# A hybrid RG-LRU and mLSTM step: the next x projection ahead of the gates, and a setup whose loads don't wait

## The chip, the core and the metric

One core of a Trainium2 chip runs the whole step as one program. The metric is the device time of that program in microseconds; smaller is better.

## What is computed

Two layers on 128 context and 1024 latent tokens of 1024 channels, in float32. The change touches the first layer's start and its recurrence only:

```python
def rms_norm(x, g):
    return x * lax.rsqrt(jnp.mean(x * x, axis=-1, keepdims=True) + EPS) * g
def ada_mod(cond, w, b):                       # w: (1024, 3072)
    return jnp.split(jax.nn.silu(cond) @ w + b, 3)      # shift, scale, gate
h = rms_norm(x, g_pre) * (1 + scale) + shift   # cond: c for latents, c_ctx for context
xa, za, xb, zb = jnp.split(h @ w_in, 4)        # 1024 columns each
xa = centred_dwconv(xa, conv_w, conv_b)        # 4 taps along the tokens
for d in range(2):                             # forward, backward
    r = sigmoid(block_diag(xa, w_r[d]) + b_r[d]); i = sigmoid(block_diag(xa, w_i[d]) + b_i[d])
    log_a = -8 * r * softplus(-lam[d]); a = exp(log_a)
    u = sqrt(-expm1(2 * log_a)) * (i * xa)     # + a * h0 at the first latent token
    h_t = a_t * h_{t-1} + u_t; ya += h
y = concat(ya * silu(za), fourier(xb) * silu(zb)) @ w_out
```

The Fourier mixer (a two-dimensional DFT of xb in groups of 128 channels, and a small product), the output projection and the second layer (mLSTM) follow.

## The kernel before

Everything lies with channels on the 128 partitions and the 1152 tokens along the free dimension. Each engine has its own instruction list; they meet at semaphores that are waited for by constants worked out.

**Projections.** A float32 product is made of three: weights and activations are split into a high and a low part, and `project` (lines 114 to 127) issues 72 matmuls (8 slices of 128 channels, 3 combinations, 3 groups of 384 tokens) into one of two groups of three PSUM banks. A weight tile of 1024x128 goes through two slots: SP loads it (`w_load`, line 94) once the tile before in that slot is split, ScalarE makes the high part (`w_split_hi`, line 100), VectorE the low part (`w_split_lo`, line 107). The tiles have one fixed order, in pairs.

**Setup** (`setup`, lines 218 to 395). SP loads x in nine tiles of 128 tokens through four slots, then w_mod in eight slices of 128 rows by 2048 columns through four slots, so it waits for the use of a slot (lines 247 and 257); then two weight tiles, the store of the transposed x to DRAM, and 13 vectors with one element per partition. ScalarE issues nine more such loads (lines 316 to 322) before its first operation. TensorE transposes x tile by tile, ScalarE and VectorE copy it to `xT`. ScalarE squares `xT` by channel slices (line 184), TensorE adds the squares up over the channels into three strips of 32 PSUM rows (line 194), root and reciprocal follow, and line 201 spreads the result over the partitions. The modulation (silu(c) and silu(c_ctx) times w_mod) is made in two ways: six slices by VectorE, which multiplies a slice by a column of the condition and adds it to a sum (line 367), two by TensorE with w_mod as the stationary operand and two moving columns (line 301); 32 + 32 one-column products add VectorE's sums over the partitions (line 307). VectorE multiplies x by the inverse deviation (line 374), adds bias and gains to the modulation (lines 377 to 381); ScalarE and VectorE then modulate x and split it (lines 216, 343, 390, 393), and the first projection follows slice by slice. A barrier of all engines ends the setup.

**Recurrence** (`lru`, lines 430 to 655): eight blocks of 128 channels. In block i TensorE projects x into group 0 and z into group 1, waits for the convolution and makes the gates, r then i for each direction (lines 507 to 524); a gate is three matmuls of 385 columns, in float32, which the profile counts as six instructions. ScalarE copies x out of PSUM (lines 545 to 547), makes the high part of a weight, takes z out by a tanh and a half (lines 552, 553) once GpSimd has finished the block before, evacuates the gates (557, 560), makes the decay (566), the tanh (570) and a square (573), splits a weight and takes two roots (584). VectorE makes the product of z (626), per direction two products (630, 632), then per direction a product and two scans (637, 640), and at the end convolves the next block's x in four operations (613, 615). GpSimd waits for the scans, adds the two directions and multiplies by z (463, 468), stores the result, and before that loads the next gate weights.

**Hand-over.** The Fourier stage (`fourier`, lines 658 to 927) has the same engines go on. TensorE projects xb of its group 0, turns it to tokens, projects zb, projects xb of group 1 and makes the token transform of group 0 (line 751), for which it waits for VectorE's eight-point butterflies. VectorE makes these after a first share of the remaining modulation (`add_modulation`, line 868), whose w_mod rows SP loads once GpSimd has finished the last block of the recurrence (line 693).

## Time and profile before

| | us |
|---|---|
| median of 3 runs | 2283.5 (2279.87 to 2286.92) |
| profiled execution, whole | 2284.8 |
| its span | 2283.2 |
| TensorE busy | 2115.9 (93%) |
| setup, to the barrier | about 104 |
| recurrence, to the last gate | 104 to 404 |

Busy times are shares of the span, and a busy TensorE is not one at its full clock: the granted clock of a stretch is given as a share of 2.4 GHz. A row of the timeline is a run of like instructions; what stands in brackets behind it is how long its engine had been idle and which instruction ended that. PE is TensorE, PEld its weight loads, DVE VectorE, ACT ScalarE, POOL GpSimd, SP the engine that issues most loads; a q behind a name stands for the engine's queue of issued work.

### The profile page before, as it was taken

The numbers are of one execution on the slowest core, as the hardware profiler recorded it, in microseconds if no ns is written. First come the engines' busy times: TensorE is split into PE (matmuls) and PEld (weight loads), VectorE is DVE, ScalarE is ACT, GpSimd is POOL, SyncE is SP. The second block draws the span as 40 slices with busy tenths as digits, with TensorE's granted clock in tenths as the row PEclk, the third lists the DMA queues.
The fourth block names the chain that finished last, engine by engine and source line by source line (L and its number), as shares of the span: only waits on it lengthen the run. The fifth ranks groups of instructions, "written<-read, shape, count | busy, mean of one in ns | idle before, by whom it ended". The sixth has DMA issues, their size and how long they took to land. (4 is left out here: it accounts for less than half of the span.)

```text
span 2283.2 us, 29516 instructions
## 1 busy us (share of the span) xinstructions
PE 2115.9 (93%) x12271; PEld 2020.3 (88%) x12271; DVE 1138.0 (50%) x1627; ACT 631.4 (28%) x710; POOL 147.0 (6%) x128
## 2 busy tenths in 40 slices
PE   5799898999999998858999999999999999989997
PEld 3778787899989998858999999999999999879997
DVE  4756666566866125666343433434343434553144
ACT  2356564421223224422121211112121211113242
POOL 0021313100000001200000000000000000000001
PEclk8699999999997999979999999999999999999998
DMA  7611111234254135312222031212222031342155
GB/s 215 163 47 47 53 47 53 66 127 133 67 169 165 41 101 164 129 46 80 70 75 63 19 110 37 90 49 83 63 75 63 26 106 33 79 175 77 56 153 179
DMA packets 235554, 205.09 MB, mean 90 GB/s; under 512 B 37306, under 2 KB 217018, under 8 KB 233266
## 3 DMA queue, kind: packets, MB, share of 16 engines
q1 hardware_dynamic: 219202, 191.07, 27.1%
q0 software_dynamic: 3680, 12.29, 1.5%
q10 hardware_dynamic: 12560, 0.12, 0.3%
q8 instruction: 85, 1.39, 0.3%
q14 instruction: 27, 0.22, 0.0%
HBM read 168.01 MB, written 35.29 MB: 89 GB/s over the span
## 5 line engine op out<-in xcount | busy, mean ns | idle before, releaser
L124 PE MATMUL psum_groups<-h_hi,w_hi 128*128 128x384 f32 x2280 | 530.9, 346 | 53.9 <-ACT q_t L1828 23.2
L124 PE MATMUL psum_groups<-h_lo,w_hi 128*128 128x384 f32 x2280 | 512.1, 337 | 0.0
L124 PE MATMUL psum_groups<-h_hi,w_lo 128*128 128x384 f32 x2088 | 480.3, 338 | 0.0
L124 PEld LDWEIGHTS psum_groups<-h_hi,w_hi 128*128 128x128 f32 x2280 | 410.9, 191 | 68.8 <-issue 37.3
L124 PEld LDWEIGHTS psum_groups<-h_lo,w_hi 128*128 128x128 f32 x2280 | 409.6, 190 | 0.0
L109 DVE TENSOR_TENSOR w_lo<-w_raw,w_hi 128x1024 fp32r<-128x1024 f32 x161 | 205.0, 1274 | 370.5 <-ACT w_hi L105 364.7
L124 PEld LDWEIGHTS psum_groups<-h_hi,w_lo 128*128 128x128 f32 x2088 | 377.3, 190 | 0.0
L105 ACT ACTIVATE w_hi<-w_raw 128x1024 fp32r<-128x1024 f32 x161 | 170.0, 1056 | 421.9 <-PE psum_groups L124 144.6
L1980 DVE SCALAR_TENSOR_TENSOR state<-state,head_decay,psum_extra 128x257 f32<-128x257 f32 x112 | 54.0, 482 | 289.4 <-PE psum_groups L1714 287.4
L1731 PE MATMUL psum_groups<-w_hi,h_hi 128*128 128x256 f32 x576 | 161.9, 281 | 2.8 <-ACT v_rows L1832 1.5
L1731 PE MATMUL psum_groups<-w_lo,h_hi 128*128 128x256 f32 x576 | 159.8, 277 | 0.0
L1731 PE MATMUL psum_groups<-w_hi,h_lo 128*128 128x256 f32 x576 | 159.8, 277 | 0.0
L145 PE MATMUL psum_groups<-h_lo,w_hi 128*128 128x384 f32 x432 | 119.0, 348 | 4.6 <-DVE w_lo L109 4.6
L145 PE MATMUL psum_groups<-h_hi,w_hi 128*128 128x384 f32 x432 | 117.1, 343 | 4.0 <-DVE h_lo L1374 2.1
L1731 PEld LDWEIGHTS psum_groups<-w_hi,h_hi 128*128 128x128 f32 x576 | 108.4, 188 | 4.8 <-ACT v_rows L1832 3.2
L1731 PEld LDWEIGHTS psum_groups<-w_hi,h_lo 128*128 128x128 f32 x576 | 108.4, 188 | 0.0
L1731 PEld LDWEIGHTS psum_groups<-w_lo,h_hi 128*128 128x128 f32 x576 | 108.2, 188 | 0.0
L522 PE MATMUL psum_groups<-xa_convolved,gate_weights 128*128 128x385 f32 x192 | 78.9, 574 | 27.3 <-DVE xa_convolved L615 23.9
L522 PEld LDWEIGHTS psum_groups<-xa_convolved,gate_weights 128*128 128x128 f32 x192 | 42.5, 226 | 61.2 <-DVE xa_convolved L615 26.1
L1083 POOL TENSOR_TENSOR square_sums<-square_sums,out_squares 128x1152 f32<-128x1152 f32 x6 | 16.0, 2674 | 1201.4 <-ACT out_squares L1238 1201.4
L1712 PE MATMUL psum_groups<-v_rows,decay_matrix 128*128 128x257 f32 x288 | 85.3, 382 | 3.5 <-DVE h_rows L1993 3.5
L1838 ACT ACTIVATE o_tanh<-psum_groups 128x1152 f32<-128x1152 f32 x16 | 18.1, 1131 | 252.3 <-PE psum_groups L124 252.3
(280 smaller groups left out, 2719.7 us busy)
## 6 DMA issues: line engine op xcount, KB each, us to landing
w_raw<-in_w_in_o SPq DMA_DIRECT2D x65, 512.0 KB, 4.4
w_raw<-in_w_in_e SPq DMA_DIRECT2D x32, 512.0 KB, 6.0
w_raw<-in_w_out_e SPq DMA_DIRECT2D x32, 512.0 KB, 3.9
w_raw<-in_w_out_o SPq DMA_DIRECT2D x32, 512.0 KB, 4.2
w_mod_rest<-in_w_mod SPq DMA_DIRECT2D x8, 1536.0 KB, 8.1
y_scratch<-mixed_y POOLq DMA_DIRECT2D x16, 576.0 KB, 5.9
h_hi<-y_scratch SPq DMA_DIRECT2D x8, 1152.0 KB, 8.8
h_lo<-y_scratch SPq DMA_DIRECT2D x8, 1152.0 KB, 15.5
```

Source lines behind the costliest of these rows:

```text
L105: act.activation(WHI[:, slot, :], WRAW[:, slot, :], ACT.Copy).then_inc(w_hi, 1)
L109: dve.tensor_tensor(WLO[:, slot, :], WRAW[:, slot, :], WHI[:, slot, :].bitcast(F32), ALU.subtract).then_inc(w_lo, 1)
L124: ins = pe.matmul(PS[:, group, j, 0:JW], w[:, slot, k * P:(k + 1) * P], h(k0 + k)[:, j * JW:(j + 1) * JW], start=start and k == 0 and m == ...
L145: ins = pe.matmul(bank, w[:, slot, k * P:(k + 1) * P], h(k0 + k)[:, g * JW:(g + 1) * JW], start=start and k == 0 and m == 0, stop=stop and ...
L522: ins = pe.matmul(PS[:, what, j, 0:JP], GW[:, 2 * what + d, :], XC[:, j * JP:(j + 1) * JP], start=True, stop=True)
L1083: pool.tensor_tensor(ACC[:], ACC[:], SQ[:].rearrange("p j n -> p (j n)"), ALU.add).then_inc(wide_added, 1)
L1712: ins = pe.matmul(NUM[d][:, 0:DV1], DM[q][:, d, cols], V[q][:, t, :], start=True, stop=s == 0)
L1731: ins = pe.matmul(dst, h[:, k, t * P:(t + 1) * P], w[:, slot, cols], start=k == 0 and m == 0 and n % 2 == 0, stop=k == KC - 1 and m == 2, ...
L1838: ins = act.activation(by_bank(TO[:]), group, ACT.Tanh, scale=0.5)
L1980: ins = dve.scalar_tensor_tensor(C[:, d, :], C[:, d, :], DC[:, d, tiles[d]:tiles[d] + 1], KV[d][:, 0:DV1], ALU.mult, ALU.add)
```

## The change

**Setup.** x gets nine slots (in the place of the later h_hi) and w_mod seven; SP issues all of x and seven slices without a wait, then the first weight tile, and the eighth slice after the first has been used. The vectors come as rows of 128 elements (five loads at the start for c, c_ctx, biases and gains; six in the middle of the squares for the recurrence), and TensorE turns each set in one transpose; SP issues none of them. ScalarE squares x by rows, with the sum over a row as a second result, right from the loaded tile; one root, one reciprocal, and nine products spread it. The modulation is TensorE's alone: for each slice four products with the two conditions (padded to 32 columns) as the stationary operand and 512 columns of w_mod as the moving one, each into its own strip of 32 PSUM rows; a copy by ScalarE and four transposes bring it to channels on partitions. VectorE's multiply-adds, the square sums on TensorE and the one-column products are gone.

**Recurrence.** TensorE projects z of block i, then x of block i + 1, then makes the gates of i, i before r in each direction. ScalarE takes out x of i + 1 at the start of block i, and z of i + 1 at its end, after the roots, into a new tile `z_tanh_a`; the tanh of the first direction waits for GpSimd's result of the block before. VectorE makes both i products, splits a weight, and puts the convolution of i + 1 between the two variances; its product of z now waits for GpSimd. Block 7 takes xb of the Fourier stage in the place of a next x, and the Fourier stage's first group projects zb ahead of the turn to tokens.

The core of the diff (most lines that go stand in the listing above and are left out here; semaphore names are changed elsewhere too):

```diff
+                src = a["x_prompt"][0] if t == 0 else a["x_sample"][0, (t - 1) * P:t * P, :]
+                sp.dma_start(XR[:, t, :], src).then_inc(x_in[t], 16)
             for n in range(KC):
                 if n >= WS:
...
+                    w_load(sp, 0, 0, in_tile(a["w_in_e"][0], 0))
+                    sp.wait_ge(wm_used, n - WS + 1)
                 sp.dma_start(WM[:, n % WS, :], wm_src[n][:, 0:2 * D]).then_inc(wm_in[n % WS], 16)
...
+            w_load(sp, 0, 1, in_tile(a["w_in_e"][0], D))
...
+            pe.wait_ge(x_rstd, 1)
+            pe.wait_ge(xT_act, 4)
+            for t in range(NT):
+                ins = pe.matmul(PS[:, 1, t // NJ, t % NJ * P:(t % NJ + 1) * P], STD[:, t:t + 1].to_broadcast([P, P]),
+                                IDENT[:], start=True, stop=True, skip_group_check=True)
+            ins.then_inc(x_spread, 1)
             pe.wait_ge(cond_ready, 1)
...
+            for k in range(KC):
                 pe.wait_ge(wm_in[k % WS], 16 * (k // WS + 1))
...
+                for j in range(4):
+                    ins = pe.matmul(PX[32 * j:32 * j + 32, 0, :], SCP[:, k, :], WM[:, k % WS, j * 512:(j + 1) * 512],
+                                    start=k == 0, stop=k == KC - 1)
                 ins.then_inc(wm_used, 1)
...
+            pe.wait_ge(mod_rows, 1)
...
+            for b in range(4):
+                ins = pe.transpose(PX[:, 1, b * P:(b + 1) * P], MR[:, b * P:(b + 1) * P], IDENT[:])
+            ins.then_inc(mod_turned, 1)
...
+                act.wait_ge(x_in[t], 16)
+                if t >= 2:
+                    act.wait_ge(x_summed, t - 1)
+                act.activation(SQ[:, t % 2, :], XR[:, t, :], ACT.Square, accum_out=SSQ[:, t:t + 1]).then_inc(x_summed, 1)
+                if t % 2 == 0 and t:
+                    x_copy(t - 1)
+            act.wait_ge(x_summed, NT)
+            act.wait_ge(zero_ready, 1)
+            act.activation(STD[:], SSQ[:], ACT.Sqrt, scale=1.0 / D, bias=EPSB[:]).then_inc(x_std, 1)
...
+            act.wait_ge(wm_used, KC)
+            act.activation(MR[:], PX[:, 0, :], ACT.Copy).then_inc(mod_rows, 1)
...
-            def block_of(i, first):
-                if not first:
-                    pe.wait_ge(r_out, i * 2)
-                    project(pe, i, 0, 0, hhi, hlo)
-                    pe.wait_ge(i_out, i * 2)
-                project(pe, i, 1, 1, hhi, hlo)
...
+            def gates(i):
                 pe.wait_ge(gw_in, i * 32 + 32)
                 pe.wait_ge(conv, i + 1)
                 for d in range(2):
...
+                    for what in (1, 0):
                         if what == 0:
...
+                            if d:
+                                pe.wait_ge(r_out, i * 2 + 1)
+                            elif isinstance(i, int) and i == KC - 1:
+                                pe.wait_ge(xb_out, 1)
+                            else:
+                                pe.wait_ge(x_out, i + 2)
                         else:
                             pe.wait_ge(*((i_out, i * 2 + 1) if d else (z_out, i + 1)))
                         for j in range(NJ):
...
                                             start=True, stop=True)
                         ins.then_inc(mm, 1)
...
+            def next_x(i):
+                project(pe, i, 0, 0, hhi, hlo)
+            project(pe, 0, 1, 1, hhi, hlo)
+            pe.wait_ge(x_out, 1)
+            next_x(1)
+            gates(0)
+            def block_of(i):
+                pe.wait_ge(i_out, i * 2)
+                project(pe, i, 1, 1, hhi, hlo)
+                pe.wait_ge(r_out, i * 2)
+                next_x(i + 1)
+                gates(i)
+            with pe.Fori(1, KC - 1) as i:
+                block_of(i)
+            block_of(KC - 1)
...
+            def z_evacuate(i, first=False):
                 projected(act, i, 1)
                 if not first:
...
+                    act.wait_ge(var1, i * 2)
+                act.activation(by_bank(ZT[:]), PS[:, 1, :, 0:JW], ACT.Tanh, scale=0.5)
                 act.activation(by_bank(ZH[:]), PS[:, 1, :, 0:JW], ACT.Copy, scale=0.5).then_inc(z_out, 1)
...
+                w_split_hi(act, i + 1, 1)
+            def block_of(i, first, last=False):
+                if last:
+                    projected(act, KC, 0)
+                    act.activation(by_bank(XB[:]), PS[:, 0, :, 0:JW], ACT.Copy).then_inc(xb_out, 1)
+                    w_split_hi(act, KC + 1, 0)
+                else:
+                    x_evacuate(i + 1)
+                if not first:
+                    act.wait_ge(scanned, i)
...
+                gate_i_out(0)
+                gate_r_out(0)
+                gate_i_out(1)
                 decay(0)
...
+                gate_r_out(1)
+                if not first:
+                    act.wait_ge(y_ready, i)
                 decay_squared(0)
                 decay(1)
                 decay_squared(1)
...
                 for d in range(2):
                     act.wait_ge(var1, i * 2 + 1 + d)
                     act.activation(T1[:, d, :], T1[:, d, :], ACT.Sqrt, scale=0.25).then_inc(root, 1)
...
+                if not last:
+                    z_evacuate(i + 1)
+            x_evacuate(0, True)
+            z_evacuate(0, True)
             block_of(0, True)
...
+            with act.Fori(1, KC - 1) as i:
                 block_of(i, False)
+            block_of(KC - 1, False, last=True)
...
+            w_split_lo(dve, 1, 0)
             convolve(0, first=True)
...
+            w_split_lo(dve, 1, 1)
+            before = ch.n
             def block_of(i, first, last=False):
...
                 dve.wait_ge(z_out, i + 1)
...
+                if not first:
+                    dve.wait_ge(y_ready, i)
+                ch.link(dve.scalar_tensor_tensor(GZ[:], ZT[:], 1.0, ZH[:], ALU.add, ALU.mult))
                 dve.wait_ge(conv, i + 1)
                 for d in range(2):
                     dve.wait_ge(i_out, i * 2 + 1 + d)
...
+                    ins = dve.scalar_tensor_tensor(T2[:, d, :], T2[:, d, :], 1.0, XC[:], ALU.add, ALU.mult)
+                ch.link(ins)
+                w_split_lo(dve, i + 2, 0)
+                for d in range(2):
                     dve.wait_ge(squared, i * 2 + 1 + d)
                     dve.scalar_tensor_tensor(T1[:, d, :], T1[:, d, :], 1.0, HT[:, d, :], ALU.add,
                                              ALU.mult).then_inc(var1, 1)
...
+                    if d == 0 and not last:
+                        convolve(i + 1)
...
             def group(i, m, slot, first):
                 channel_weights(m, slot)
+                if not first:
+                    pe.wait_ge(ua_out, i)
+                    project(pe, i + KC, 0, 0, hhi, hlo)
+                    token_transform(i - 1)
+                if first:
+                    pe.wait_ge(i_out, 2 * KC)
+                    project(pe, i + KC, 1, 1, hhi, hlo)
+                pe.wait_ge(xb_out, i + 1)
+                pe.wait_ge(cw_out, m * 2 + slot + 1)
                 if first:
                     pe.wait_ge(r_out, 2 * KC)
                 else:
...
                     pe.wait_ge(ub_out, i)
                 to_tokens(0, 6, lambda t: PS[:, 0, t // 2, t % 2 * 256:t % 2 * 256 + 256], ua_done)
                 to_tokens(6, 9, lambda t: PX[:, t // 2, t % 2 * 256:t % 2 * 256 + 256], ub_done)
...
+                if not first:
                     pe.wait_ge(y_ready, i)
...
+                    project(pe, i + KC, 1, 1, hhi, hlo)
```

## Rows read from the trace of the kernel before

**Rows 1.** The page, part 1: busy time and share of each engine.
```profile
PE 2115.9 (93%) x12271; PEld 2020.3 (88%) x12271; DVE 1138.0 (50%) x1627; ACT 631.4 (28%) x710; POOL 147.0 (6%) x128
```

**Rows 2.** Windows: busy us (instructions) per engine, granted clock, DMA share, GB/s.
```profile
27.00:34.00 7.00, 3.25 (x24) 2.57 (x24) 2.78 (x4) 2.24 (x3) 0.00 (x0) 1.00 0.92 327
...
34.00:44.00 10.00, 8.08 (x48) 1.50 (x48) 6.90 (x5) 9.40 (x9) 0.00 (x0) 0.83 0.98 407
...
48.00:60.00 12.00, 8.70 (x40) 7.54 (x37) 12.00 (x6) 0.00 (x0) 0.00 (x0) 0.50 0.42 143
...
88.00:104.00 16.00, 15.40 (x72) 14.97 (x72) 12.16 (x13) 11.80 (x12) 0.00 (x0) 0.82 0.00 1
...
129.50:156.00 26.50, 25.20 (x145) 24.88 (x144) 20.41 (x16) 13.97 (x14) 8.38 (x6) 1.00 0.10 30
```

**Rows 3.** Timeline of the setup: start, us, engine, line, operation, count, idle before.
```profile
47.57 18.09 DVE L367 SCALAR_TENSOR_TENSOR mod_sums<-w_mod_rows,cond_silu,mod_sums 128x2048 f32<-128x2048 f32 x8
...
69.04 13.79 PE L307 MATMUL psum_extra<-ones,mod_sums 128*128 128x1 f32 x64
...
83.59 1.62 ACT L216 ACTIVATE norm_tmp<-x_normed,mod_shift,mod_scale 128x128 f32<-128x128 f32 x2 [18.58 <-DVE mod_scale L381]
```

**Rows 4.** Timeline, ScalarE in the setup: a load's issue, a table load, a copy.
```profile
1.50 0.60 ACTq L317 DMA_DIRECT2D cond<-in_c_ctx  x1
...
17.51 1.28 ACT L324 ACT_TABLE_LOAD   x1 [17.51 <-issue]
...
24.39 1.02 ACT L327 ACTIVATE xT<-psum_groups 128x1024 f32<-128x1024 f32 x1 [4.46 <-PE psum_groups L288]
```

**Rows 5.** Groups by line, 0 to 560 us: busy us, mean ns, idle before.
```profile
L615 DVE SCALAR_TENSOR_TENSOR xa_convolved<-xa_padded,lru_params,xa_convolved 128x1155 f32<-128x1155 f32 x24 | 56.7, 2363 | 2.9 <-DVE xa_convolved L613 0.9 <-DVE xa_convolved L615 0.9
...
L640 DVE TENSOR_TENSOR_SCAN tanh_then_state<-decay,lru_params,gate_i 128x1024 f32<-128x1024 f32 x16 | 37.2, 2325 | 0.0
...
L109 DVE TENSOR_TENSOR w_lo<-w_raw,w_hi 128x1024 fp32r<-128x1024 f32 x26 | 33.4, 1284 | 30.1 <-ACT w_hi L105 30.1
...
L630 DVE SCALAR_TENSOR_TENSOR gate_i<-gate_i,xa_convolved 128x1155 f32<-128x1155 f32 x16 | 21.7, 1358 | 30.3 <-ACT gate_i L560 30.3
...
L374 DVE TENSOR_TENSOR x_normed<-xT,psum_groups 128x1152 f32<-128x1152 f32 x8 | 10.2, 1347 | 0.0
```

**Rows 6.** DMA issues, 0 to 130 us: count, KB each, median us to landing.
```profile
w_mod_rows<-in_w_mod SPq DMA_DIRECT2D x8, 1024.0 KB, 7.5
...
norm_gains<-in_g_post ACTq DMA_DIRECT2D x2, 4.0 KB, 4.0
```

**Rows 7.** Timeline of TensorE: squares' sums, gates after a project, gates after a wait.
```profile
39.86 0.85 PE L194 MATMUL psum_extra<-squares,ones 128*32 128x384 f32 x6 [0.21 <-ACT squares L184]
...
121.11 2.11 PE L522 MATMUL psum_groups<-xa_convolved,gate_weights 128*128 128x385 f32 x6
...
161.67 3.90 PE L522 MATMUL psum_groups<-xa_convolved,gate_weights 128*128 128x385 f32 x6 [3.17 <-ACT z_half L553]
```

**Rows 8.** Timeline of the recurrence: the convolution alone; GpSimd's sums and who waits.
```profile
113.78 4.34 DVE L615 SCALAR_TENSOR_TENSOR xa_convolved<-xa_padded,lru_params,xa_convolved 128x1155 f32<-128x1155 f32 x3
...
189.14 3.32 POOL L463 TENSOR_TENSOR tanh_then_state<-tanh_then_state 128x128 f32<-128x128 f32 x2 [17.52 <-DVE lru_final L642]
...
197.19 1.28 ACT L552 ACT_TABLE_LOAD   x1 [12.76 <-POOL mixed_y L468]
```

**Rows 9.** Timeline: the last block's gates and the hand-over to the Fourier stage.
```profile
393.95 9.73 PE L522 MATMUL psum_groups<-xa_convolved,gate_weights 128*128 128x385 f32 x24 [3.71 <-DVE xa_convolved L615]
...
423.14 3.72 POOL L463 TENSOR_TENSOR tanh_then_state<-tanh_then_state 128x128 f32<-128x128 f32 x2 [29.10 <-DVE lru_final L642]
...
429.39 25.33 SPq L686 DMA_DIRECT2D w_mod_rest<-in_w_mod  x4
...
438.09 2.35 DVE L868 TENSOR_SCALAR mod_by_partition<-w_mod_rest,cond_silu 128x4096 f32<-128x4096 f32 x1 [13.89 <-DMA w_mod_rest<-in_w_mod]
...
450.29 3.84 PE L751 MATMUL psum_groups<-token_dft,transformed 128*128 128x128 f32 x32 [2.87 <-DVE transformed L827]
```

More of the change, by code:

```diff
@@ L198, in spread_pe @@
-    def spread_pe(pe, n, group=0):
-        pe.wait_ge(rstd_ready, n + 1)
-        for j in range(NJ):
-            ins = pe.matmul(PS[:, group, j, 0:JW], ONES[32 * j:32 * j + 1, :], RSTD[32 * j:32 * j + 1, :],
-                            start=True, stop=True)
-        ins.then_inc(rstd_spread, 1)
-    def stats_dve(dve, n, used, count):
-        dve.wait_ge(used, count)
-        dve.tensor_scalar(RSTD[:], PX[0:96, 1, 0:JW], 1.0 / D, EPS, ALU.mult, ALU.add).then_inc(var_ready, 1)
-        dve.wait_ge(std_ready, n + 1)
-        dve.reciprocal(RSTD[:], RSTD[:]).then_inc(rstd_ready, 1)
+        sp.dma_start(dst, y_dram[2 * n:2 * n + 2].rearrange("k p t -> p k t")).then_inc(rows_in[n], 16)
@@ L314, in _, with rows, by_row, x_copy @@
         def _(act):
[L315 to L325 removed]
+            def rows(n, first, src, done):
+                act.dma_start(VR[first:first + src.shape[0], n, :], src).then_inc(done, 16)
+            def by_row(x):
+                return x.rearrange("l (k p) -> (l k) p", p=P)
+            def x_copy(t):
                 act.wait_ge(x_turned, t + 1)
@@ L515, in block_of @@
                 for d in range(2):
-                    for what in range(2):
+                    for what in (1, 0):
                         if what == 0:
-                            pe.wait_ge(*((r_out, i * 2 + 1) if d else (x_out, i + 1)))
+                            if d:
[4 more added lines that the diff above has]
+                                pe.wait_ge(x_out, i + 2)
                         else:
@@ L540, in on_scalar, with x_evacuate @@
             act.wait_ge(prm_ready, 1)
-            def block_of(i, first):
+            def x_evacuate(i, first=False):
                 projected(act, i, 0)
@@ L593, in on_vector @@
             w_split_lo(dve, 0, 1)
-            dve.wait_ge(prm_in, 16 * 13)
+            dve.wait_ge(prm_in, 1)
             dve.wait_ge(lam_exp, 1)
@@ L963, in build @@
     y_summed, y_std, y_rstd, y_spread = (sem(s) for s in ("y_summed", "y_std_ready", "y_rstd_ready", "y_rstd_spread"))
-    residual_in = [sem(f"residual_loaded_{g}") for g in range(NJ)]
     scaled = sem("out_normed")
```

258 lines of the change are left out of this document (97 added, 161 removed).

## The prediction

> **What bounds the kernel now.** I read the page first: TensorE is busy for 93% of the span [rows 1], so time comes back only where TensorE stands still or runs at its lower clock. The windows by stage, read next, show two such places, and they are the two stages that the change touches. In the setup (0 to 104 us) one of the stretches in which TensorE forms the modulation sums, 48 to 60 us, has a granted clock of 0.50, which is 1.2 of 2.4 GHz; its last 16 us hold the first projection [rows 2]. In the recurrence (107 to 404 us) two projections keep it busy for 25.2 us [rows 2], and then it waits. I then followed both stages in the timeline. The setup ends on the modulation chain: VectorE's multiply-adds of w_mod run until 65.7 us, 64 one-column products bring the sums across partitions until 82.8, and only at 83.59 may ScalarE, idle for 18.6 us, modulate x [rows 3]. In the recurrence the gates of every block but the first wait: before the last block's, TensorE is idle for 3.71 us until the convolution is done, and the 24 gate instructions then take 9.73 us [rows 9]. A quarter of them, six, took 2.11 us straight after a projection, but 3.90 after an idle 3.17 [rows 7]: the wait costs once more, through the clock. First gates of block 0 at 121.11, of block 7 at 393.95 [rows 7, 9]: seven periods of 38.98 us.
>
> **The setup, step by step.** I time the new order by the old rows.
> Vectors: ScalarE issues five loads at 0.60 us each from 1.0 on [rows 4], and the last lands 4.0 us later [rows 6], at 8.0 (at the 7.5 of a large load, 11.5). A turn on TensorE, a table load of 1.28 [rows 4] and two small operations bring 10.3. (The two-element cond loads go, and with them ScalarE's nine slow issues: its table load stood at 17.51 [rows 4].)
> ScalarE then has nine row squares and four copies of 128x1024 at 1.02 us [rows 4], and six more load issues in their midst, 3.6 us: 13.3 + 3.6, until 27.2. I count nothing for the added sum over a row; it has no row, the bound is one more small operation of 0.2 us each, 1.8 us. VectorE's copies run beside this. The root with its table load gives 28.7, reciprocal and nine spreading products, by the 0.35 us of one gate instruction [rows 7], 32.2.
> VectorE normalises: eight of 1.28 us (10.2 in all, [rows 5]) and a weight split of 1.28, until 43.7.
> TensorE meanwhile: 8 x 4 products are 64 instructions of 512 columns. A gate instruction of 385 columns takes 0.35 us [rows 7], so one of 512 some 0.45, and 64 in a row 28.8. The four of a slice write different 32-row strips. The row nearest to it is that of the square sums, whose six instructions of 384 columns in three strips took 0.85 us together, drain included, where six gate instructions took 2.11 [rows 7]: the strips run side by side. So 16 times 0.45, 7.2 us at the full clock, 14.4 at the half: from 32.2 to 39.4 or 46.6. The eighth slice is still loaded behind a wait, once the first is used, at about 33.5, and takes 7.5 to land [rows 6], so 41.5, plus its 0.9. I take 44, between the two clocks.
> For this chain x and w_mod, some 13 MB (nine loads of 512 KB, eight of 1024), must be in by then. At the 407 GB/s of the stretch 34 to 44 us they take 33 us, at 327 GB/s 41 [rows 2]; both fit.
> One copy out, four transposes and the small operations: 0.6 + 1.3 + 0.8, the last from 82.83 to 83.59 [rows 3]. The chain's end comes at **46.7** instead of 83.59: **36.9 us gained**. Its ends: VectorE's floor 43.7 + 0.8 gives 39 us; half clock and late vectors, 53, give 30.
> What follows it (modulation, projection, barrier) is unchanged. The 4.7 MB store of x is issued later, but ends some 20 us before the barrier. The 13 vector loads at the end of SP's queue were covered by the projection: nothing for them.
> By the granted clock, TensorE was at its full level while it transposed at 27 to 34 us [rows 2]. The Trainium skill (TensorE: Matmul & The Clock Gate, Part 4) says that transposes do not release the clock. By the row, the products may start at the full level; by the page they would start at the half one, and the chain would end at 49.3 instead of 46.7, by estimate. The row speaks against the page.
>
> **The recurrence.** The projection of the next x moves ahead of the gates, z stays. TensorE's order is now z(i), x(i+1), gates(i), and the convolution of i is finished a block earlier. Block 0 gets one more projection before its gates, 12.6 us: they start at 133.7 in the old axis. A period is then 25.2 for the projections [rows 2] plus 8.1 for the gates, four times 2.11 less overlapping ends [rows 7]: 33.3 us.
> Does anything else take its place? From the start of the gates (0): x is evacuated in 1.5, ScalarE splits a weight, then reads the first i gate at 2.6 to 3.8; the second i gate needs that and begins at 4.0, when the first r gate ends. Exponential, tangents and squares end at 12.4 and 16.3. VectorE's convolution goes between the two variances: 13.9 to 19.7 (four of 1.45 by [rows 8], where GpSimd is idle). Roots at 23.2, z evacuated behind them at 25.8. Scans end at about 29.5 (a 1.36 product and 2.6 for 1155 columns, twice, by [rows 5]), GpSimd's sums at 37.5 (8.05 from [rows 8]). The next gates, at 33.3, need z (25.8) and the scans (29.5): covered by 7.5 and 6.4 us. GpSimd's result is first needed by VectorE's z product and by ScalarE's tangent 10 us into the block: covered by 5. If the cover goes, the period is that chain's.
> Block 7's gates start at 133.7 + 7 x 33.3 = 366.8: 27.2 earlier than 393.95. From there I follow what ended last before: scans at +29.2, GpSimd, the load of w_mod that waits for it, its landing at 438.09, and VectorE's add and eight-point transform, on which TensorE waited 2.87 us until 450.29 [rows 9]. This chain keeps its length, but for the gates' 1.6 us: TensorE goes on at 421.5, **28.8 us earlier**. It has less to do meanwhile: 46.6 us of work and wait lay between 403.7 and 450.29 [rows 9], now one projection of 12.6 and the old wait less, 31.1, from 374.9 to 406. So **a new idle time of 15.5 us** stands before the token transform. That is why a stage that loses over 39 us of TensorE time gives 28.8. After it TensorE should run at its lower clock for a while; by [rows 7] six instructions lose 1.8 us, I take 1.5.
>
> **Sum.** The profiled execution took 2284.8 us (span 2283.2), 1.3 above the median of 2283.5. 2284.8 - 36.9 - 28.8 + 1.5 = **2220.6**, predicted 2221.
>
> **Rivals.**
> A. The strips run one after the other: 28.8 us instead of the 11.8 counted, so the chain ends 17 us later, 2238; at half clock throughout 57.6, 2266. Against it stands [rows 7], three strips in 0.85 us; it is not shown for four strips.
> B. The chain through VectorE and GpSimd bounds a block. Summed by rows: five products of 1.36, a split of 1.28, the convolution of 5.8, or 9.5 at the mean of 2.36 beside GpSimd, the scans 7.9, a root wait of 1, GpSimd 6.25 (423.14 to 429.39, [rows 9]) or 8.05 [rows 8]: 29.0 to 34.5. At the upper end a period is 1.2 longer, 2229; with 2 us more of waits between engines, 2243. For it: this loop is close to TensorE's 33.3. Against it: GpSimd now runs where VectorE has nearly nothing.
> C. The loads without waits hold up ScalarE's six issues behind 13 MB: it stands until some 42 us with 11 us of squares and copies left, the products start at 58, the chain ends at 70: 2244. For it: all queues share the DMA engines, 0.98 busy at 34 to 44 us [rows 2]. Against it: the loads of [rows 6] landed in 4.0 us beside x.
> D. Slower than before. z is evacuated behind the roots, and these behind ScalarE's wait for GpSimd's sums of the block before; the gates wait for z. It decides from 7.5 us of lateness on, and the kernel is slower only if a period passes 33.3 + 64.2/7 = 42.5 us: GpSimd's sums would have to take some 30 us instead of 8.05. Nothing in the trace is near that.
>
> **How the numbers follow.** Forecast 0.70, A 0.08, B 0.10, C 0.09, D 0.02, quicker than 2207 0.01. The forecast's own ends: 39 us in the setup, a last load that lands 4 us sooner and no clock loss give 2213; 30 us in the setup and 3 more of clock loss 2230. A measurement of this kernel can tell about 0.3%, 7 us, from no change. The range, 2207 to 2244, takes in B, C and A at full clock, and leaves out A at half and D. Faster 0.96, same 0.02, slower 0.02.
>
> **What would show it.** Right: ScalarE's first modulation near 47 us; four strips' products starting together; gates straight after a projection, about 8 us, in blocks 33 apart; one idle time of some 15 us before the token transform, ended by VectorE. Wrong: 64 products in over 25 us (A); TensorE idle in front of gates on ScalarE or VectorE (B); ScalarE's issues long in the middle of the squares (C). The forecast fails if the chain of the setup ends after 60 us or a period passes 36.

## The result, and the profile after

The changed kernel takes 2218.8 us (median of four runs, 2216.4 to 2222.4) beside 2283.9 for the kernel before: a ratio of 0.9717, with a 95% interval of 0.9695 to 0.9740. The forecast was 2221, the range 2207 to 2244. The profiled execution took 2216.4 us (span 2214.7). The number came out, but with two terms in it that the prediction did not have, 12.6 us gained and 15.4 us lost, which nearly cancel. Most of what follows is about these.

On the page, part 1 (busy time and share of each engine), TensorE has gone from 93% [rows 1] to 94% of a span that is 68.5 us shorter:

```profile
PE 2087.9 (94%) x12175; PEld 2008.2 (91%) x12175; DVE 1086.3 (49%) x1615; ACT 632.9 (29%) x727; POOL 133.5 (6%) x128
```

**The setup.** The timeline of after (start, us, engine, line, operation, count, idle time before it), to be read beside [rows 3]:

```profile
22.76 1.28 ACT L304 ACT_TABLE_LOAD   x1
...
28.27 5.54 PE L254 MATMUL psum_extra<-w_mod_rows,cond_silu_columns 128*32 128x512 f32 x48
34.64 1.06 PE L254 MATMUL psum_extra<-w_mod_rows,cond_silu_columns 128*32 128x512 f32 x8 [0.82 <-DMA w_mod_rows<-in_w_mod]
38.87 1.91 PE L254 MATMUL psum_extra<-w_mod_rows,cond_silu_columns 128*32 128x512 f32 x8 [3.16 <-DMA w_mod_rows<-in_w_mod]
...
28.38 10.21 DVE L344 TENSOR_TENSOR x_normed<-xT,psum_groups 128x1152 f32<-128x1152 f32 x8 [3.76 <-PE psum_groups L246]
...
43.36 1.62 ACT L172 ACTIVATE norm_tmp<-x_normed,mod_shift,mod_scale 128x128 f32<-128x128 f32 x2 [1.93 <-DVE mod_scale L353]
```

The six slices that had landed took 5.54 us for 48 instructions: the four strips of a slice run side by side. Then TensorE waits for data, 3.16 us for the eighth slice. ScalarE modulates x at 43.36 us instead of 83.59.

**The recurrence and the hand-over**, again the timeline, to be read beside [rows 9]:

```profile
94.87 7.93 PE L497 MATMUL psum_groups<-xa_convolved,gate_weights 128*128 128x385 f32 x24
...
324.17 7.94 PE L497 MATMUL psum_groups<-xa_convolved,gate_weights 128*128 128x385 f32 x24
...
350.93 2.80 POOL L438 TENSOR_TENSOR tanh_then_state<-tanh_then_state 128x128 f32<-128x128 f32 x2 [22.87 <-DVE lru_final L662]
...
365.56 2.35 DVE L888 TENSOR_SCALAR mod_by_partition<-w_mod_rest,cond_silu 128x4096 f32<-128x4096 f32 x1 [14.73 <-DMA w_mod_rest<-in_w_mod]
...
377.77 6.64 PE L770 MATMUL psum_groups<-token_dft,transformed 128*128 128x128 f32 x32 [14.47 <-DVE transformed L847]
```

No gates wait, and their 24 instructions take 7.93 us. Block 0 and block 7 lie 229.30 us apart, seven periods of 32.76. The new idle time stands where it was expected: 14.47 us before the token transform.

**Where the time went**, by landmarks of the two profiled executions. The first token transform starts 72.5 us earlier (450.29 to 377.77): 40.2 of these are the setup's, 32.3 come between. The eighth and last token transform starts 85.1 us earlier (695.4 to 610.3), so the Fourier stage gave another 12.6. The first value product of the mLSTM stage starts 83.9 us earlier (1022.5 to 938.6), and the end comes only 68.5 earlier: 15.4 us were given back in a stage that the diff does not touch. With the 1.2 us that were lost between the last token transform and that product, 2284.8 - 40.2 - 32.3 - 12.6 + 1.2 + 15.4 = 2216.3. The last three terms are not in the prediction.

The Fourier stage first. The waits in five of its groups (line waited for, sum in us, times, longest), before at 483 to 660 us:

```profile
ACT w_hi L105 <- DMA w_raw<-in_w_in_e: 82.2, 5, 17.1
...
DVE w_lo L109 <- ACT w_hi L105: 51.0, 5, 11.1
...
PE psum_groups L124 <- DVEq L889: 4.5, 4, 1.2
```

and after at 414 to 580 us:

```profile
ACT w_hi L106 <- DMA w_raw<-in_w_in_e: 31.8, 5, 7.9
DVE mixed_y L905 <- PE psum_groups L773: 27.6, 5, 7.5
DVE w_lo L110 <- ACT w_hi L106: 10.4, 4, 3.5
```

Before, TensorE waited for VectorE's outputs (L889) and VectorE for weights; after, VectorE waits for TensorE (L905). SyncE's issues of w_mod_rest, which wait for VectorE's last addition of a group, show the pace. Before and then after:

```profile
523.37 0.99 SPq L686 DMA_DIRECT2D w_mod_rest<-in_w_mod  x2
...
661.98 0.97 SPq L686 DMA_DIRECT2D w_mod_rest<-in_w_mod  x2
```

```profile
413.58 0.87 SPq L705 DMA_DIRECT2D w_mod_rest<-in_w_mod  x2
...
576.23 0.87 SPq L705 DMA_DIRECT2D w_mod_rest<-in_w_mod  x2
```

Before: four groups in 138.6 us, 34.7 each. After: five in 162.7, 32.5 each, with TensorE's transforms 33.3 apart. That gave the **rhythm theory**: the loop from SyncE's loads over ScalarE's split, VectorE's additions and butterflies back to SyncE either runs ahead of TensorE, which then sets 33.3 us, or behind it, and then sets 34.7 itself. Its rival, the **sum theory**, counts each wait by itself. (Where the expectations below give the Fourier stage 251.5 us in before and 239 in after, they count to the end of the eighth transform, 6.4 us more than the tables here, which count from start to start.)

### The profile page after: what moved, and what is told of

Read it like the earlier page. It is cut to its first block and busy times, and to the rows that moved or that the text cites. A ratio compares the mean times of both kernels' runs of the same rounds, so it can differ in the third digit from the quotient of the medians.

```text
span 2214.7 us, 29333 instructions
## 1 busy us (share of the span) xinstructions
PE 2087.9 (94%) x12175; PEld 2008.2 (91%) x12175; DVE 1086.3 (49%) x1615; ACT 632.9 (29%) x727; POOL 133.5 (6%) x128
## 5 line engine op out<-in xcount | busy, mean ns | idle before, releaser
L125 PEld LDWEIGHTS psum_groups<-h_hi,w_hi 128*128 128x128 f32 x2280 | 413.8, 191 | 60.7 <-issue 27.4
L125 PEld LDWEIGHTS psum_groups<-h_lo,w_hi 128*128 128x128 f32 x2280 | 411.6, 189 | 0.0
L110 DVE TENSOR_TENSOR w_lo<-w_raw,w_hi 128x1024 fp32r<-128x1024 f32 x161 | 202.9, 1261 | 326.7 <-ACT w_hi L106 320.1
L146 PEld LDWEIGHTS psum_groups<-h_lo,w_hi 128*128 128x128 f32 x432 | 82.0, 198 | 5.0 <-DVE w_lo L110 5.0
L146 PEld LDWEIGHTS psum_groups<-h_hi,w_hi 128*128 128x128 f32 x432 | 79.2, 190 | 6.0 <-issue 4.4
```

The costliest lines, as they stand in the source:

```text
L110: dve.tensor_tensor(WLO[:, slot, :], WRAW[:, slot, :], WHI[:, slot, :].bitcast(F32), ALU.subtract).then_inc(w_lo, 1)
L125: ins = pe.matmul(PS[:, group, j, 0:JW], w[:, slot, k * P:(k + 1) * P], h(k0 + k)[:, j * JW:(j + 1) * JW], start=start and k == 0 and m == ...
L146: ins = pe.matmul(bank, w[:, slot, k * P:(k + 1) * P], h(k0 + k)[:, g * JW:(g + 1) * JW], start=start and k == 0 and m == 0, stop=stop and ...
```

## The experiments

Medians, and landmarks of each profiled execution (us): start of ScalarE's first modulation, start of the first token transform, time from the first to the eighth token transform, time from the first value product of the mLSTM stage to the end of the span.

| kernel | median | modulation | first transform | Fourier | mLSTM to end |
|---|---|---|---|---|---|
| before | 2283.9 | 83.6 | 450.3 | 245.1 | 1260.7 |
| after | 2218.8 | 43.4 | 377.8 | 232.5 | 1276.1 |
| setup_only | 2255.6 | 44.5 | 410.2 | 244.8 | 1273.7 |
| recurrence_only | 2239.6 | 82.5 | 415.1 | 232.6 | 1261.9 |
| butterflies_first | 2217.7 | 43.3 | 363.6 | 253.4 | 1277.0 |
| both_first | 2207.5 | 43.9 | 364.4 | 240.0 | 1275.9 |
| additions_late | 2203.4 | 43.8 | 362.7 | 234.0 | 1276.6 |
| conv_last | 2253.1 | 43.2 | 413.1 | 232.6 | 1276.9 |
| eight_slots | 2215.1 | 44.2 | 383.1 | 232.6 | 1276.5 |
| one_strip (one run) | 2226.1 | 54.6 | 389.0 | 232.6 | 1277.0 |
| zone_as_before | 2200.2 | 44.7 | 381.7 | 232.7 | 1262.0 |
| pad_64 | 2210.2 | 43.4 | 376.2 | 232.5 | 1273.1 |
| before_plus_64 | 2300.4 | 84.3 | 451.8 | 246.7 | 1277.0 |
| best | 2186.9 | 44.5 | 364.8 | 231.0 | 1261.9 |

Two columns hold the findings. The Fourier time goes by who is ahead in the first group. The last column is 1261 to 1262, or 1273 to 1277, and goes by where the tiles lie.

**The two halves, each alone.** setup_only:

```diff
-lru(), fourier() of after
+lru(), fourier() of before
```

> The new setup with the recurrence and Fourier stages of before. Both theories of the Fourier stage expect the whole 40.2 us that the first modulation came earlier (83.59 to 43.36): about 2244 us. The sum theory (every wait counts by itself) and the rhythm theory (in the Fourier stage either TensorE or the loop of loads, splits and additions on VectorE sets the pace, 33.4 or 35.8 us a group) both leave the Fourier stage as in before, 251.5 us from its first token transform to its last. If the 15 us that the mLSTM stage lost after the change belong to the setup, the time is about 2255 us instead.

Measured 2255.6 us, ratio to before 0.9873 (0.9827 to 0.9920). The first token transform comes 40.1 us earlier, the Fourier stage is as slow as before's, and the mLSTM stage takes 1273.7 us instead of 1260.7. The second case, then: what after lost late **belongs to the setup**. (The profiled execution was the longest of the four, at 2262.3; 5 of its microseconds lie between the last token transform and the mLSTM stage.)

recurrence_only:

```diff
-setup() of after
+setup() of before
```

> The old setup with the new recurrence and Fourier stages. The sum theory expects the 32.3 us that lie between the first modulation and the first token transform (72.5 less 40.2) and no more: about 2252 us. The rhythm theory expects the quick rhythm of the Fourier stage besides, 239 us instead of 251.5 between its first and last token transform, so 2239 us if the mLSTM stage gives nothing back, and 2250 to 2254 us if it does.

Measured 2239.6 us, ratio 0.9819 (0.9778 to 0.9860). The Fourier stage takes the quick rhythm, 232.6 us, and the mLSTM stage gives nothing back. The sum theory's 2252 is out. The two halves' gains, 26.2 and 42.2 us beside the 2281.8 of before measured with them, add up to 68.4, about the 65.1 of the whole change.

**The idle time of 14.5 us.** butterflies_first, on VectorE:

```diff
 def group(i, last=False):
...
-    add_modulation(i, 0)
+    first = isinstance(i, int) and i == 0
+    if not first:
+        add_modulation(i, 0)
...
     eight_points(i)
     gate(i)
+    if first:
+        add_modulation(i, 0)
```

> After, with the butterflies and the gate of the first Fourier group ahead of the first addition of the second modulation on VectorE, so that TensorE's 14.5 us of idle time before the first token transform goes. The sum theory expects that idle time and the 2.8 us of the half clock behind it back: 2203 to 2206 us. The rhythm theory expects TensorE to be some 10 us further ahead of VectorE's loop than in after; the stores of y then fall beside the loads of w_raw again, TensorE waits about 1 us a group for VectorE's outputs, the groups take 35.8 us, and the gain is given back: 2216 to 2226 us, with 247 us or more from the first to the last token transform.

Measured 2217.7 us (2217.5 to 2221.3): nothing gained. The transform starts at 363.6 us, 14.2 earlier, with 1.7 us of waiting instead of 14.47; then everything is given back. The second transform is still 6.3 us earlier than in after (407.7), the eighth 6.7 later (617.0). Its waits at 407 to 580 us read like before's:

```profile
ACT w_hi L106 <- DMA w_raw<-in_w_in_e: 79.1, 5, 16.4
...
DVE w_lo L110 <- ACT w_hi L106: 49.6, 5, 10.2
...
PE psum_groups L125 <- DVEq L909: 3.3, 4, 1.1
```

SyncE's issues go from 411.33 to 584.34 in five groups, 34.6 us each, and first to last transform is 253.4 us. The rhythm theory had said 2216 to 2226 and 247 or more, the sum theory 2203 to 2206. The theory's figure of 35.8 us a group was taken from one interval of before and was too high by 1.2.

both_first adds this on SyncE:

```diff
     w_mod_rows(0)
+    w_load(sp, KC + 2, 0, ...)
     sp.wait_ge(mod_part, 2)
     w_mod_rows(1)
-    with sp.Fori(1, KC - 1) as i:
-        w_load(sp, i + KC + 1, 0, ...)
+    with sp.Fori(1, KC - 2) as i:
         w_load(sp, i + KC + 1, 1, ...)
+        w_load(sp, i + KC + 2, 0, ...)
         sp.wait_ge(mod_part, i * 2 + 2)
         w_mod_rows(i + 1)
...
```

> The same, and SyncE issues each group's load of the x weights ahead of its wait for the addition of the modulation, one group earlier, so that the split of the weights no longer waits behind the 2 MB of w_mod_rest. The rhythm theory expects TensorE to set the pace although it is ahead: 33.4 us a group, no waits for VectorE's outputs, about 2203 us. The sum theory expects no more than from butterflies_first alone, 2203 to 2206 us; if both come out alike, the rhythm theory has fallen.

Measured 2207.5 us, ratio 0.9676 (0.9635 to 0.9716), 10.2 us better than butterflies_first: the two did not come out alike. From the second on the transforms are 33.3 us apart although TensorE starts as early. What stands out in the gap to 2203 is one wait, in group 1 (timeline of both_first):

```profile
380.83 1.33 PE L125 MATMUL psum_groups<-h_hi,w_hi 128*128 128x384 f32 x3 [8.24 <-DVEq L913]
```

The outputs of group 0 stand behind the two additions on VectorE, and these wait for 2 MB of w_mod_rest. additions_late puts the two additions behind the outputs, in group 1 (the first lines are VectorE's, beside after; the last are SyncE's, beside both_first):

```diff
-    add_modulation(i, 0)
+    if not isinstance(i, int) or i > 1:
+        add_modulation(i, 0)
+    elif i == 1:
+        add_modulation(0, 0)
+        add_modulation(0, 1)
...
+    w_load(sp, KC + 2, 0, ...)
     sp.wait_ge(lru_y_ready, KC)
     w_mod_rows(0)
-    w_load(sp, KC + 2, 0, ...)
```

> As both_first, but both additions of the second modulation's first slice stand behind the outputs of the first Fourier group on VectorE, and the first of the early x weight loads is issued ahead of SyncE's wait for the recurrence. The rhythm theory expects the 8.2 us wait for VectorE's outputs in group 1 and the half clock behind it to go, so that the second token transform comes at 397 to 400 us instead of 408.7, and all groups take 33.4 us: 2195 to 2199 us. If the wait only moves on to the next group, 2205 to 2208.

Measured 2203.4 us (2198.3 to 2204.7), ratio 0.9650 (0.9623 to 0.9676). The wait is 2.50 us instead of 8.24, the second transform starts at 400.4, the stage takes 234.0. The time lies between the two cases, 4 us above the first one's upper end, and 2.50 us of the wait are still there. The profiled execution's span is 12.8 us below after's.

**The recurrence's cover.** conv_last, on VectorE:

```diff
 for d in range(2):
...
-    if d == 0 and not last:
-        convolve(i + 1)
...
 if not last:
+    convolve(i + 1)
     w_split_lo(dve, i + 2, 1)
```

> After, with the convolution of the next block back at the end of VectorE's block, behind the scans; x still comes ahead of the gates. If the earlier place of the convolution is what took the wait away, the gates wait again, 1 to 4 us in each of seven blocks, with the slower gates behind them: 2230 to 2250 us. If x ahead of the gates is enough by itself, the convolution ends before TensorE is through with z and the next x, the period stays 32.8 us and the time 2219 to 2222 us.

Measured 2253.1 us, ratio 0.9864 (0.9835 to 0.9892), 34 us worse than after and above the upper end of what either case allowed. Its timeline, one block:

```profile
154.86 3.33 POOL L438 TENSOR_TENSOR tanh_then_state<-tanh_then_state 128x128 f32<-128x128 f32 x2 [16.98 <-DVE lru_final L660]
...
156.09 3.32 DVE L628 SCALAR_TENSOR_TENSOR xa_convolved<-xa_padded,lru_params,xa_convolved 128x1155 f32<-128x1155 f32 x1 [0.16 <-DVE xa_convolved L626]
159.57 4.50 DVE L628 SCALAR_TENSOR_TENSOR xa_convolved<-xa_padded,lru_params,xa_convolved 128x1155 f32<-128x1155 f32 x2 [0.16 <-DVE xa_convolved L628]
...
164.17 10.90 PE L497 MATMUL psum_groups<-xa_convolved,gate_weights 128*128 128x385 f32 x24 [3.48 <-issue]
203.50 9.70 PE L497 MATMUL psum_groups<-xa_convolved,gate_weights 128*128 128x385 f32 x24 [3.45 <-issue]
```

The convolution falls beside GpSimd's sums; there its three multiply-adds take 7.8 us, in after 4.4, and end 0.1 us before the gates start. From the third block on the gates wait 3.4 to 3.5 us, and take 9.4 to 11.0 instead of 7.9. The two gates shown are 39.3 us apart, and the period from the third block to the last is 38.6 us on average, nearly before's 38.98. The first token transform comes at 413.1 us, no sooner than in setup_only (410.2). **x ahead of the gates, with the other reorderings, gains nothing by itself; the place that it makes free for the convolution does.** The prediction had both in its list and did not weigh them apart.

**The modulation's end.** eight_slots:

```diff
+w_lo_at = bottom[0]
...
-WS = 7
+WS = 8
...
-SQ = sb("squares", [P, 2, D], at=z)
+SQ = sb("squares", [P, 2, D], at=[w_lo_at])
...
 for n in range(KC):
-    if n >= WS:
-        w_load(sp, 0, 0, ...)
-        sp.wait_ge(wm_used, n - WS + 1)
     sp.dma_start(WM[:, n % WS, :], ...)
+w_load(sp, 0, 0, ...)
 w_load(sp, 0, 1, ...)
```

> After, with eight slots for w_mod instead of seven (the squares' tile shares the place of w_lo), so that the eighth slice is loaded without a wait and ahead of the first projection's weights. The load theory (the modulation chain ends on the eighth slice's landing, for which TensorE waited 3.16 us) expects the first modulation at 40.5 to 41.5 us instead of 43.36 and 2216 to 2217 us. If VectorE's normalisation, which ended at 39.7, is what bounds it by then, no earlier than 40.7. If the wait was covered anyway: 43.4 and 2219 us.

Measured 2215.1 us (2212.1 to 2220.1), not to be told from after. The modulation came at 44.2 us, later than in after: a miss of all three. Its timeline:

```profile
28.76 4.50 PE L253 MATMUL psum_extra<-w_mod_rows,cond_silu_columns 128*32 128x512 f32 x40
33.66 1.07 PE L253 MATMUL psum_extra<-w_mod_rows,cond_silu_columns 128*32 128x512 f32 x8 [0.40 <-DMA w_mod_rows<-in_w_mod]
...
38.99 1.93 PE L253 MATMUL psum_extra<-w_mod_rows,cond_silu_columns 128*32 128x512 f32 x8 [1.54 <-DMA w_mod_rows<-in_w_mod]
...
40.75 1.06 ACT L107 ACTIVATE w_hi<-w_raw 128x1024 fp32r<-128x1024 f32 x1 [15.62 <-DMA w_raw<-in_w_in_e]
41.71 0.58 ACT L312 ACTIVATE mod_rows<-psum_extra 128x512 f32<-128x512 f32 x1
```

The eighth slice lands no sooner (38.99 beside 38.87) though nothing holds its issue, which now lies before 12.5 us instead of at 29.59. In both runs the DMA share is about 1.0 from 12 us until it lands: it was the bytes, and not the slot. What the 0.5 MB of weights that no longer lie ahead of it are worth can't be read from this pair, since this execution moved fewer bytes (387 to 391 GB/s from 20 to 36 us, after 379 to 428), and its seventh slice was used 1.7 us later already (36.38 beside 34.64). (Five slices take 4.50 us, one alone 1.07 with its drain: 0.86 from slice to slice.) And the first weights, now last in line, hold ScalarE up ahead of its copy of the sums, which starts at 41.71 us instead of 40.83.

one_strip:

```diff
+pe.wait_ge(xT_dve, 5)
...
 for j in range(4):
-    ins = pe.matmul(PX[32 * j:32 * j + 32, 0, :], ...)
+    dst = PX[32 * j:32 * j + 32, 0, :]
+    if k < KC - 1:
+        dst = PX[0:32, 0, :] if j == 0 else PS[0:32, 0, j - 1, :]
+    ins = pe.matmul(dst, ..., start=k in (0, KC - 1), stop=k >= KC - 2)
```

> After, with the four products of each of the first seven slices of w_mod written to the same 32 rows of four banks instead of four strips of one bank (only the last slice then counts in the modulation, so the output is another). Rival A's price by itself: with eight instructions of 0.43 us one after the other a slice takes 3.4 us at the full clock instead of 0.86, the seven take 24 us, and the first modulation comes at 55 to 58 us instead of 43.4: 2230 to 2233 us. If the strips were never side by side, nothing changes: 43.4.

Measured 2226.1 us in one run. Eight instructions of a slice in its timeline:

```profile
27.35 1.04 PE L258 MATMUL psum_extra<-w_mod_rows,cond_silu_columns 128*32 128x512 f32 x2
28.23 2.74 PE L258 MATMUL psum_groups<-w_mod_rows,cond_silu_columns 128*32 128x512 f32 x6
30.81 1.02 PE L258 MATMUL psum_extra<-w_mod_rows,cond_silu_columns 128*32 128x512 f32 x2
```

3.46 us from slice to slice instead of 0.86, and the modulation at 54.6 us, 11.2 later (55 to 58 expected). Rival A's mechanism was real, and the strips are what kept it away.

**The 64 bytes.** The new setup keeps 96 vector columns in one tile where before had 80 in two. The 16 more, of 4 bytes each, put every tile declared behind it 64 bytes higher on each partition, those of the later stages too. zone_as_before:

```diff
-LAM = sb("lru_lambda", [P, 2, KC])
+LAM = VT[:, 0:16].rearrange("p (d k) -> p d k", d=2)
...
-act.activation(LAM[:], turned[:, 88:104]...)
+act.wait_ge(cond_ready, 1)
+act.activation(LAM, turned[:, 88:104]...)
```

> After, with the 64 bytes of lambda kept in 64 bytes of the new vector tile that are free by then, so that every tile declared behind it (h2 and all of the later stages) stands where it stood in before; after has them 64 bytes higher. Address theory: the 128x256 products of the values in the mLSTM stage take 277 ns again instead of 282 and the 128x384 projections there 336 instead of 338, and the stage gets back 10 to 12 us: 2207 to 2209 us. If the slower products come from elsewhere in the new setup: 282 ns and 2219 us, as after.

Measured **2200.2 us** (2199.9 to 2201.6), ratio 0.9641 (0.9618 to 0.9664): 18.6 us better than after. That is more than the 10 to 12 expected; by the spans it is 14.6, of which the mLSTM column shows 14.1.

pad_64 and before_plus_64 are one line each, in after and in before:

```diff
+sb("pad", [P, 16])
```

> After, with another 64 bytes left free behind the vector tile, so that every later tile stands 64 bytes higher than in after and 128 higher than in before. If what counts is the address modulo 128, the 128x256 products take 277 ns as in before and the time is 2200 to 2204 us; if it is the tiles' one old place or their address modulo 256 or more, 282 ns and 2219 us.

> Before, with 64 bytes left free behind the norm gains and nothing else changed, so that every later tile stands where it stands in after. The address theory expects the mLSTM stage to lose what after lost there, 282 instead of 277 ns for the 128x256 products: 2293 to 2300 us beside 2282 to 2284. If the new setup does it in another way: no change.

before_plus_64 took 2300.4 us, ratio 1.0086 (1.0058 to 1.0113): the kernel before, slowed by 20 us through 64 unused bytes (16.0 by the spans, and 16.3 in the mLSTM column). pad_64 took 2210.2 (2205.5 to 2213.1), and answers to neither of its two cases: it lies between. The value products of the mLSTM stage, by line (durations min/median/max in ns, first and last start), in before, after, zone_as_before, pad_64 and before_plus_64:

```profile
L1731 PE MATMUL psum_groups<-w_lo,h_hi x576: 276/276/286, 1022.7 to 1881.1; 128*128 128x256 f32 x192
```

```profile
L1751 PE MATMUL psum_groups<-w_lo,h_hi x576: 274/281/287, 938.8 to 1811.4; 128*128 128x256 f32 x192
```

```profile
L1752 PE MATMUL psum_groups<-w_lo,h_hi x576: 276/276/286, 938.3 to 1798.2; 128*128 128x256 f32 x192
```

```profile
L1752 PE MATMUL psum_groups<-w_lo,h_hi x576: 276/280/282, 931.1 to 1800.5; 128*128 128x256 f32 x192
```

```profile
L1732 PE MATMUL psum_groups<-w_lo,h_hi x576: 274/282/287, 1022.4 to 1895.1; 128*128 128x256 f32 x192
```

Not a few slow products, then, but the median: 276 ns at the old place, 281 and 282 with 64 bytes, 280 with 128. All 1728 value products together are busy for 488.7 us in after and 481.5 in zone_as_before, and the 3800 products of 384 columns at line 125, from 935 us on, for 883.2 and 874.0: both kinds are slower, and together they account for the 14.1 us between these two kernels. That the address does it is shown from both sides. Which address of which tile, and why, stays open: it is not simply the remainder by 128.

**Both gains together.** best is additions_late with zone_as_before's edit.

> additions_late and zone_as_before together. If the two gains are independent, the 15.4 us of additions_late (2218.8 to 2203.4) and the 18.6 of zone_as_before (2218.8 to 2200.2) add up to 2185 us; by the profiled executions alone (12.8 and 14.6 us of the span) 2190. If the pace of the mLSTM stage depends on when it starts and not on the addresses, no better than 2200.

Measured **2186.9 us** (median of five, 2180.6 to 2192.1), ratio to before 0.9587 (0.9561 to 0.9613). The gains add up to within 2 us: they are independent. That is 31.9 us below after (2218.8, not measured beside it), about half of what the change itself gave.

## Why the prediction was right, and where it was not

**The number is right by more than its reasons.** Predicted 64.2 us of gain, measured 68.5 in the profiled executions. The predicted places gave 72.5; two places for which the sum has no term gave 12.6 and took 15.4, and 1.2 went between them. That these nearly cancel is luck: zone_as_before, which is the change without the 15.4, took 2200.2 us, below the predicted range.

**The setup: right, and closer to its bound than the sum had it.** 36.9 us predicted, 40.2 measured. The vectors landed at 7.9 us (8.0 predicted). ScalarE's six load issues in the midst of the squares, counted at 3.6 us, took 0.32 to 0.44 each, beside the running squares, and left ScalarE idle for no more than 0.50. The last copy ended at 22.7 us instead of 27.2. What had no row, the reading of the added sum, was an instruction of 0.19 us, at the bound given. The products did as the strips' row said. The prediction took 44 us, "between the two clocks"; what ended last was neither clock but the eighth slice, used at 40.8. The prediction had that slice land at 41.5, held up by its slot; its products started at 38.87, and what held it up was the bytes. Rival C did not come: no issue stalled.

**The clock in the setup.** By the row, TensorE was to start the products at the full level after its transposes; by the Trainium skill (TensorE: Matmul & The Clock Gate, Part 4) transposes do not release the clock. Windows of after (busy us of PE, PEld, DVE, ACT and POOL, granted clock, DMA share, GB/s):

```profile
20.00:22.00 2.00, 1.93 (x17) 1.71 (x17) 0.24 (x2) 2.00 (x5) 0.00 (x0) 1.00 1.05 442
...
26.00:28.00 2.00, 2.00 (x11) 2.00 (x10) 0.00 (x0) 0.00 (x0) 0.00 (x0) 0.50 0.98 414
...
29.00:34.00 5.00, 4.81 (x48) 1.12 (x40) 5.00 (x5) 0.00 (x0) 0.00 (x0) 1.00 1.03 396
```

Full while it transposes, half (1.2 GHz) for the spreading products behind an idle time of 2.73 us, full again from 29 us. In conv_last, with the same setup and the same 2.73 us of idle time, the clock stayed at 1.00:

```profile
26.00:28.00 2.00, 2.00 (x20) 1.37 (x22) 0.69 (x1) 0.00 (x0) 0.00 (x0) 1.00 1.00 422
```

So the row is no rule, and the page's sentence doesn't foretell it either. In after TensorE kept the full level while it did nothing but transpose (1.00 from 8 to 22 us); it had that level before its first transpose, so whether transposes can raise the clock is not shown. The half clock of the spreading products cost nothing in the end, since the chain ended on a load. The half clock behind the wait for that load did cost: the eighth slice's eight instructions took 1.91 us, at a granted clock of 0.51, where those of the slice before took 1.06 at 1.00, and these 0.85 us stand in the chain.

**The recurrence: the mechanism right, 3.5 us short.** The hand-over was predicted 28.8 us earlier than the setup alone makes it, and came 32.3 earlier. The period is 32.76 us against 33.3: the overlap of gates and projections was underestimated, which gives seven times 0.54, 3.8 us. The chain behind the last gates was 1.1 shorter than taken (53.6 us from gates to token transform, 54.7 predicted). Against that, block 0's gates came at 94.9 us, 1.9 before the 96.8 predicted (133.7 - 36.9) where the setup had come 3.3 earlier: 1.4 were lost there. Rival B did not come. conv_last shows what held it off: with the convolution beside GpSimd the four operations take 9.1 us, near the 9.5 that the rival reckoned with, and the period is 38.6 where the rival's sum ends at 34.5. Its chance of 0.10 rested on the convolution's place. Rival D's "some 30 us" is too low: by the prediction's own steps GpSimd's sums would have to take about 40 us for a period of 42.5. They took 6.3, so nothing hangs on it.

**The new idle time: right.** 15.5 us predicted, 14.47 measured, on the chain named. The half clock behind it cost 2.8 us instead of 1.5: the 32 transforms took 6.64 us where they took 3.84 before [rows 9].

**What the sum lacks is any term for what follows the hand-over.** (1) In the Fourier stage TensorE's start against VectorE's loop was changed, and with it the rhythm of all eight groups: +12.6 us. Five groups gave 1.2 each on average; the half clock in the first group took 2.8; the last group gave 9.4. There TensorE no longer waits 3.3 us for VectorE's additions, and the 64 one-column products, which stood at the half clock behind that wait, run at the full one until about 605 us. Before and then after:

```profile
681.34 13.78 PE L790 MATMUL psum_groups<-ones,mod_by_partition 128*128 128x1 f32 x64 [3.27 <-DVE mod_by_partition L871]
```

```profile
600.99 9.49 PE L809 MATMUL psum_groups<-ones,mod_by_partition 128*128 128x1 f32 x64
```

The 14.5 us of idle time were the price of it: butterflies_first takes them away and ends where after ends. (2) In the mLSTM stage the tiles lay 64 bytes higher: -15.4 us. No view of before could show this, but the diff did: it declares a tile of 96 columns in place of 80. Had only the second happened, the time would have been near 2229; only the first, near 2201, outside the range.

**Argued, not shown:** that the slow rhythm is slow because VectorE's outputs, when they are not kept waiting, send the store of y beside the load of weights. In the groups counted above the traces have the store's issue 1.9 to 2.3 us behind that of the load in before, 2.4 to 2.5 in butterflies_first, and 6.5 to 10.1 in after; no run moved the store alone. The 5 us ahead of the mLSTM stage in setup_only were not followed up.

## What to carry to other kernels

An idle time at a seam can hold two loops in a favourable order: before filling it, look at which engine waits for which in the steady state on both sides, and loosen the loop first, here by issuing loads ahead of the wait that they do not need. Moving one operation off a shared stretch (the convolution away from GpSimd's sums) did what the reordering of TensorE's own work would have been credited with; the reordering only made the place for it. And when a change alters the size of a tile that is declared early, compare the instruction times of the stages it does not touch, and pin the addresses if they move.

## What the runs showed of the hardware

- **SBUF addresses set the pace of products.** 64 bytes more in front of the tiles made the 128x256 products 281 to 282 ns instead of 276, 128 bytes 280; a program of 2280 us became one of 2300. The granted clock from 1100 to 1900 us is 0.99 to 1.00 in all of them.
- **Four strips at once.** Eight instructions of 512 columns in four strips take 0.86 us, one strip 3.46: the fourfold, also for float32.
- **ScalarE issues loads while it computes.** Six issues of 0.32 to 0.44 us lay beside squares of 1.05 and left 0.50 us of idle time; the five at the start of the program took 0.28 to 0.60. The sum over a row is an instruction of 0.19 us behind each square: square follows square after 1.04 us.
- **VectorE and GpSimd slow each other.** Multiply-adds of the convolution took 1.4 to 1.5 us alone and up to 3.3 beside GpSimd's sums, and the products with z on GpSimd took 4.5 us instead of 2.4.
- **The granted clock after transposes is not fixed.** 0.50 or 1.00 behind the same 2.73 us of idle time, in two executions of the same setup.
